# A hybrid encoder layer on one core: half of branch C's output gate is projected later, between the merges of two branches

## The chip, the cores and the metric

One core of one Trainium2 chip runs one launch of the kernel. The metric is the device time in microseconds (us), the median of several runs. TensorE is called PE, VectorE DVE, ScalarE ACT, GpSimd POOL and SyncE SP, as in the profile.

## The reference, cut to what matters

One encoder layer over 512 tokens of width 1024, in float32. A normed input n is projected once; three token mixers (A: sparse attention, B: stick-breaking attention, C: gated linear attention) work on the columns; their outputs are merged under sigmoid gates; a second block retrieves 16 experts for each of 8 heads and each token.

```python
# branch C: o is the output of the recurrence, r the columns cr of n @ w_in
o = rms_norm(o, out_gain) * jax.nn.silu(r)
...
merged = gates[:, :, 0] * (ya @ w_oa) + gates[:, :, 1] * (yb @ w_ob) + gates[:, :, 2] * (yc @ w_oc)
return merged @ w_out
...
# the expert block, for each block of 128 tokens
u = u_tab[expert]
vv = v_tab[expert]
act = gelu(einsum('nd,nhkd->nhk', xb, u))
out = einsum('nhk,nhkd->nd', g * act, vv)
```

The change concerns r, the output gate of branch C: 512 columns, 1024 inputs, 512 tokens. It is needed only as silu(r), multiplied into the normed output of branch C.

## The kernel before, in words

The order of the work is written out by hand, engine by engine. There are two stages.

**The front** runs until the first expert rows are fetched. PE projects n through a list of jobs (`jobs_of_projection`, one job being eight matmuls of 128x512, line 662 for jobs with tokens in the columns, line 664 for jobs with tokens in the rows). The last jobs of the list are four for r (name "rc", one for each 128 tokens) and two for the forget gates ("cu", line 675). A job number J_A on is interleaved with the heads of branch A: `job_after(it)` puts one behind every second step `it`, and the last LATE = 4 jobs stand behind the first scores of branch B (line 805). Between the last heads of A stand also the column sums of the modulation (`column_sums`, line 598) at `it == NA + 1`, and the turn of A's output (line 748). ACT copies every job's result out of PSUM, then applies Silu to all of rc (line 1380); POOL multiplies it by the output gain (line 2200); DVE multiplies branch C's normed output by it (line 1867). After branch C, PE merges the three branches for tokens 0 to 255 (`gate_product` line 769, `out_product` line 783), projects the merged columns (`output`, line 941) and turns tokens.

**The gather stage** works through NL = 512 expert rows for 128 tokens each. POOL fetches row n (1 MB) by an indirect DMA (line 2227) into a ring of 8 places, later 10 and more; DVE takes the dot product (line 2060), ACT the Gelu and a diagonal matrix (lines 1492 and 1503), PE adds the weighted row to an accumulator (`weigh`, line 1111), except for the rows that DVE adds itself (line 2084). A place is free again when its row has been added. Four rows make a slot; there are 128 slots, and PE, ACT, DVE and SP hang the rest of the layer on them by tables of slot numbers:

- `MERGE_SLOT`: 24 merges for tokens 256 to 511 in slots 3 to 35. Merge n is `merge_products(n)` on PE (line 1013, eight matmuls of 128x256 for the gate; line 1018, four for the branch's output), `half_gate(n)` on ACT (a tanh), `half_merge(n)` on DVE (lines 1903 and 1907). Its weights (768 KB) come from SP (`merge_weights`, line 537) into one of three places.
- `PIECE_SLOT`: the output projection of these tokens (line 1037), slots 37 to 40, then the residual sum, the norm and its shift (ADD_AT 42 to SHIFT_AT 49; the shift is line 1576 on ACT).
- `LATE_QUERY_AT` (line 1047), `late_at` (attention of branch A for tokens 256 to 511, lines 1125, 1136, 1148) and `QUERY_SLOT` (expert queries, line 974, scores line 999, with 1152 KB of weights from SP, line 531).
- `KEPT_UNTIL`: the row from which two more ring places are used.

## Time and profile before

| what | value |
|---|---|
| median of 3 runs | 2058.62 us (2057.96 to 2058.76) |
| the profiled execution's own time | 2061.57 us |
| its span, first to last instruction | 2059.8 us |
| PE busy | 1671.6 us (81%) |
| DVE busy | 1457.2 us (71%) |
| ACT busy | 580.0 us (28%) |
| POOL busy | 616.0 us (30%) |
| bytes moved by DMA | 659.79 MB |
| mean granted PE clock | 0.913 of full |

The profiled execution is 1.8 us longer than its span and 3.0 us longer than the median. Shares of busy time are averages over two stages that have different limits, so the stage has to be read before the share is used. fp32 matmuls leave two records each: a job of eight matmuls has 16 records.

### The profile page before, as it was taken

The page shows a single profiled execution, that of the slowest core. Times are in us where ns is not written, and L with a number is a line of the kernel's source. Part 1 is how long each engine was busy: PE and PEld are TensorE (multiplying, and loading weights), DVE is VectorE, ACT ScalarE, POOL GpSimd, SP SyncE. Part 2 cuts the span into 40 slices and gives each one's busy share as a digit, 9 for nine tenths or more (in the row PEclk, how much of TensorE's full clock was granted, in tenths as well). Part 3 has the DMA queues.
Part 4 walks back from the last instruction along what each step waited for, and adds up shares of the span by engine and source line. Part 5 has one row for each costly group of instructions (what it writes and reads, how often), then busy time and mean ns, then how long its engine had stood idle before and what let it go on. Part 6 is the DMA issues. An engine that isn't in the chain of part 4 may idle for free.

```text
span 2059.8 us, 17894 instructions
## 1 busy us (share of the span) xinstructions
PE 1671.6 (81%) x5626; PEld 945.6 (46%) x5626; DVE 1457.2 (71%) x3371; ACT 580.0 (28%) x1272; POOL 616.0 (30%) x542
## 2 busy tenths in 40 slices
PE   4999999999898998998898667777887676666665
PEld 3533455667786665565555323333443222222222
DVE  5454642668328688877787998887777878887876
ACT  2121114664224443542222223222222222212221
POOL 0000000110003333333444445444443544344441
PEclk8999899999999999999999978888888888888988
DMA  9632120021448899999999999999999999999995
GB/s 371 247 125 89 70 102 9 31 92 62 169 163 353 336 401 417 397 403 401 412 401 419 420 419 383 420 419 420 420 419 421 420 420 419 420 419 420 420 420 243
DMA packets 89184, 659.79 MB, mean 320 GB/s; under 512 B 9968, under 2 KB 10240, under 8 KB 15488
## 3 DMA queue, kind: packets, MB, share of 16 engines
q0 software_dynamic: 73728, 536.90, 63.5%
q1 hardware_dynamic: 14768, 120.75, 14.7%
q8 instruction: 45, 0.74, 0.1%
q10 hardware_dynamic: 592, 0.98, 0.1%
q14 instruction: 51, 0.42, 0.1%
HBM read 655.52 MB, written 2.82 MB: 320 GB/s over the span
## 4 chain that ended last, share of the span: by engine, by line
DMA 39%; PE 34%; DVE 14%; issue 7%; ACT 4%; POOL 2%; SPq 0%; DVEq 0%; POOLq 0%; ACTq 0%
DMA sb<-uv_table,sb 36%; PE ps L1111 9%; PE ps L662 4%; PE ps L664 4%; DMA sb<-w_mod 3%; DVE sb L2060 3%; PE ps L769 3%; PE ps L974 2%; DVE sb L2084 2%; POOL sb L2227 2%; PE ps L1013 1%; PE ps L1018 1%; PE ps L941 1%; PE ps L783 1%; PE ps L634 1%
## 5 line engine op out<-in xcount | busy, mean ns | idle before, releaser
L1111 PE MATMUL ps<-sb 128*128 128x512 f32 x1424 | 767.7, 683 | 291.7 <-ACT sb L1503 286.9
L2227 POOL DMA_INDIRECT sb<-uv_table,sb x512 | 589.0, 1150 | 910.5 <-PE ps L1111 700.6
L2060 DVE CUSTOM_DVE_ANT_0 sb<-sb 128x1024 f32<-128x1024 f32 x512 | 625.2, 1221 | 250.3 <-DMA sb<-uv_table,sb 240.6
L1111 PEld LDWEIGHTS ps<-sb 128*128 128x128 f32 x1424 | 289.7, 216 | 717.4 <-ACT sb L1503 415.9
L1503 ACT ACTIVATE sb<-sb 128x128 f32<-128x128 f32 x356 | 132.0, 397 | 614.0 <-DVE sb L2069 607.1
L2084 DVE SCALAR_TENSOR_TENSOR sb<-sb 128x512 f32<-128x512 f32 x304 | 214.8, 748 | 2.2
L1492 ACT ACTIVATE sb<-sb 128x2 f32<-128x2 f32 x256 | 51.7, 202 | 400.1 <-DVE sb L2060 400.0
L2189 POOL TENSOR_TENSOR sb<-sb 128x128 f32<-128x128 f32 x8 | 13.1, 1636 | 427.3 <-DVE sb L1766 427.3
L662 PE MATMUL ps<-sb 128*128 128x512 f32 (+1 forms) x304 | 128.6, 576 | 0.1
L974 PE MATMUL ps<-sb 128*128 128x256 f32 (+1 forms) x576 | 123.6, 371 | 0.0
L974 PEld LDWEIGHTS ps<-sb 128*128 128x128 f32 x576 | 104.2, 204 | 29.6 <-issue 17.4
L769 PE MATMUL ps<-sb 128*128 128x256 f32 x384 | 89.9, 387 | 8.5 <-DVEq L1742 3.6
L664 PE MATMUL ps<-sb 128*128 128x512 f32 x192 | 90.3, 626 | 0.0
L662 PEld LDWEIGHTS ps<-sb 128*128 128x128 f32 x304 | 58.3, 198 | 64.2 <-issue 57.7
L1013 PE MATMUL ps<-sb 128*128 128x256 f32 x384 | 87.3, 379 | 0.0
L769 PEld LDWEIGHTS ps<-sb 128*128 128x128 f32 x384 | 71.9, 192 | 22.4 <-issue 7.4
L1013 PEld LDWEIGHTS ps<-sb 128*128 128x128 f32 x384 | 71.2, 189 | 15.1 <-issue 6.0
L1018 PE MATMUL ps<-sb 128*128 128x256 f32 x192 | 49.9, 405 | 13.7 <-DVE sb L1907 13.7
L664 PEld LDWEIGHTS ps<-sb 128*128 128x128 f32 x192 | 37.7, 201 | 47.5 <-issue 46.6
L1554 ACT ACT_TABLE_LOAD x43 | 55.2, 1283 | 0.8
L2069 DVE TENSOR_TENSOR sb<-sb 128x2 f32<-128x2 f32 x256 | 39.9, 156 | 16.8 <-ACT sb L1492 15.1
L1018 PEld LDWEIGHTS ps<-sb 128*128 128x128 f32 x192 | 37.7, 200 | 22.6 <-DVE sb L1907 16.9
(283 smaller groups left out, 1784.9 us busy)
## 6 DMA issues: line engine op xcount, KB each, us to landing
sb<-w_mod SPq DMA_DIRECT2D x11, 2048.0 KB, 9.2
sb<-w_pq SPq DMA_DIRECT2D x18, 1152.0 KB
sb<-w_merge SPq DMA_DIRECT2D x24, 768.0 KB
sb<-w_proj SPq DMA_DIRECT2D x8, 2048.0 KB, 8.8
sb<-w_merge SPq DMA_DIRECT2D x6, 2304.0 KB, 9.0
sb<-w_out SPq DMA_DIRECT2D x8, 1024.0 KB, 11.7
sb<-uv_table,sb POOLq DMA_INDIRECT x512, 27.8
sb<-w_merge SPq DMA_DIRECT2D x3, 1536.0 KB, 6.7
```

The costliest lines, as they stand in the source:

```text
L662: mm = pe.matmul(bank(b, n), w[:, i, k, :], n_t[:, k, 0:n], start=(k == 0), stop=(k == KT - 1))
L664: mm = pe.matmul(bank(b), n_t[:, k, P * i:P * (i + 1)], tiles(views[slot], KT)[:, k, :], start=(k == 0), stop=(k == KT - 1))
L769: mm = pe.matmul(gate_at(n), w[:, P * k:P * (k + 1)], n_t[:, k, 0:H], start=(k == 0), stop=(k == KT - 1))
L974: mm = pe.matmul(bank(6 if q < EARLY_Q else 4, n, H * c), w[:, c, k, :], n_t[:, k, lo:lo + n], start=(k == 0), stop=(k == KT - 1))
L1013: mm = pe.matmul(bank(6, H), w[:, P * k:P * (k + 1)], n_t[:, k, H:T], start=(k == 0), stop=(k == KT - 1))
L1018: mm = pe.matmul(bank(7, H), w[:, P * (KT + k):P * (KT + k + 1)], y_of(br, 1)[:, k, :], start=(k == 0), stop=(k == 3))
L1111: mm = pe.matmul(bank(2 * (t % 2) + f), dgw[m % NDG], row_v(n)[:, T * f:T * (f + 1)], start=(i == 0), stop=(i == PH * PK - 2))
L1503: act.activation(dgw[m % NDG], ident, ACT.Copy, scale=wgt[n // PK % 2][:, n % PK:n % PK + 1])\
L1554: act.activation(warm, cact[:, 0:1], ACT.Gelu)
L2060: dve.tensor_tensor_reduce(out=row_u(n), in0=row_u(n), in1=n2_tm(u // PH), scale=1.0, scalar=0.0, op0=ALU.mult, op1=ALU.add, accum_out=dot ...
L2084: ins = dve.scalar_tensor_tensor(acc_v[f], v, wgt[u % 2][:, i:i + 1], acc_v[f], ALU.mult, ALU.add)
L2227: pool.indirect_dma_start(out=ring[PLACE[n]], out_offset=None, in_=uv_table, in_offset=bass.IndirectOffsetOnAxis(ap=experts[u % 4][:, i:i ...
```

## The change

- Jobs of rc: two instead of four (tokens 0 to 255). The list is two shorter, so no job stands behind steps 17 and 19 of branch A any more, and the four late jobs are rc 0, rc 1 and the two cu jobs. Silu, the gain and DVE's product cover half the columns.
- For tokens 256 to 511 r is computed transposed in the gather stage: `ITEMS` is eight merges of branch B, four items "gate", eight merges of C, eight of A. A gate item is eight matmuls of 128x256 on PE, a tanh on ACT, and two operations on DVE, which multiply branch C's output in place. Its weights are 512 KB from a new input w_rc; the 2 MB of the front's load are as before.
- The 28 items stand in slots 4 to 37, and what follows them moves by two or three slots. The late queries and branch A's late attention move by two slots. Expert query 10 moves from slot 29 to 44, query 11 from 51 to 53.

```diff
-    jobs += [("t", 7, t, "rc", None) for t in range(TT)]
+    jobs += [("t", 7, t, "rc", None) for t in range(TT // 2)]
...
-        KEPT_UNTIL = 116
+        KEPT_UNTIL = 120
...
-        QUERY_SLOT = {4 * (q - 3) + 1: q for q in range(3, 11)}
-        QUERY_SLOT.update({(51 if q == 11 else 4 * q + 9): q for q in range(11, NQ)})
+        QUERY_SLOT = {(44 if q == 10 else 4 * (q - 3) + 1): q for q in range(3, 11)}
+        QUERY_SLOT.update({(53 if q == 11 else 4 * q + 9): q for q in range(11, NQ)})
...
-        def half_unit(n):
-            return (n // KT + 1) % 3, n % KT
+        ITEMS = [(1, c) for c in range(KT)] + [("gate", c) for c in range(4)] + [(2, c) for c in range(KT)] + [(0, c) for c in range(KT)]
+        NM = len(ITEMS)
...
         def late_at(j):
-            return 1 + j + (3 if j >= HA else 0)
+            return 3 + j + (3 if j >= HA else 0)
...
-            [3, 4, 7, 8, 11, 12, 15, 16, 19, 20, 21, 22, 23, 24, 26, 27, 28, 29, 30, 31, 32, 33, 34, 35])}
-        PIECE_SLOT = {37 + p: p for p in range(4)}
-        TURN_SLOT = {25: (6, 7), 46: (8, 9), 48: (10, 11), 53: (12, 13), 54: (14, 15)}
-        G2_SLOT = 28
-        LATE_QUERY_AT = {0: 2, 2: 3}
-        LATE_SQ_AT, LATE_VAR_AT, LATE_ROOT_AT, LATE_R_AT = 3, 4, 5, 6
-        ADD_AT, SQUARE_AT, SUM_AT, NVAR_AT, ROOT_AT, NORM_AT, SHIFT_AT = 42, 42, 44, 47, 47, 49, 49
-        ONES_AT = 45
+            [4, 6, 7, 8, 11, 12, 14, 15, 16, 18, 19, 20, 22, 23, 24, 25, 26, 27, 28, 29, 30, 31, 32, 33, 34, 35, 36, 37])}
+        PIECE_SLOT = {39 + p: p for p in range(4)}
+        TURN_SLOT = {27: (6, 7), 48: (8, 9), 50: (10, 11), 55: (12, 13), 56: (14, 15)}
+        G2_SLOT = 29
+        LATE_QUERY_AT = {2: 2, 4: 3}
+        LATE_SQ_AT, LATE_VAR_AT, LATE_ROOT_AT, LATE_R_AT = 5, 6, 7, 8
+        ADD_AT, SQUARE_AT, SUM_AT, NVAR_AT, ROOT_AT, NORM_AT, SHIFT_AT = 44, 44, 46, 49, 50, 52, 52
+        ONES_AT = 47
...
+                if br == "gate":
+                    sp.dma_start(mh_slot[n % 3][:, 0:KT * P], w_rc[:, KT * P * c:KT * P * (c + 1)]).then_inc(mh_in[n % 3], 16)
...
                 pe.wait_ge(s["gate_ready"], NG + n)
+                if n >= 1 and ITEMS[n - 1][0] == "gate":
+                    pe.wait_ge(s["gate_used"], NG + n)
...
+                if br == "gate":
+                    pe.wait_ge(s["gl_done"], NG + n + 1)
+                    pe.sem_inc(s["ob_done"], 1)
+                    pe.sem_inc(s["mh_used"], 1)
+                    return
...
-            act.activation(area("rc", 0, TT * T), area("rc", 0, TT * T), ACT.Silu).then_inc(s["rsil"], 1)
+            act.activation(area("rc", 0, 2 * T), area("rc", 0, 2 * T), ACT.Silu).then_inc(s["rsil"], 1)
...
+                if br == "gate":
+                    y = y_of(2, 1)[:, c, :]
+                    done(dve.scalar_tensor_tensor(gates_h[n % 2], gates_h[n % 2], 1.0, bank(6, H), ALU.add, ALU.mult))
+                    dve.scalar_tensor_tensor(y, y, vcol(V_OGC + c), gates_h[n % 2], ALU.mult, ALU.mult).then_inc(s["gate_used"], 1)
```

PE at the end of branch A and the start of branch B, before the change (line 664 is a job of rc, 598 the column sums, 748 the turn of A's output, 805 the first scores of B, 675 the jobs of cu):

```order
L739 MATMUL ps<-sb 128x64 x4
L664 MATMUL ps<-sb 128x512 x8
L598 MATMUL ps<-sb 128x1 x32
L748 MATMUL ps<-sb 128x128 x4
L664 MATMUL ps<-sb 128x512 x8
L805 MATMUL ps<-sb 128x512
L805 MATMUL ps<-sb 128x384
L805 MATMUL ps<-sb 128x256
L805 MATMUL ps<-sb 128x128
L664 MATMUL ps<-sb 128x512 x16
L675 MATMUL ps<-sb 128x512 x2
```

The same place in the changed kernel, whose lines are two to four numbers further on:

```order
L742 MATMUL ps<-sb 128x64 x4
L601 MATMUL ps<-sb 128x1 x32
L751 MATMUL ps<-sb 128x128 x4
L808 MATMUL ps<-sb 128x512
L808 MATMUL ps<-sb 128x384
L808 MATMUL ps<-sb 128x256
L808 MATMUL ps<-sb 128x128
L667 MATMUL ps<-sb 128x512 x16
L678 MATMUL ps<-sb 128x512 x2
```

One job ahead of the column sums and one ahead of B's first scores are gone; behind the scores stand 16 matmuls as before.

PE in slots 0 to 3 of the gather stage, before the change (1111 weighs rows, 1047 is a late query of A, 974 half an expert query, 999 its scores, 1013 and 1018 a merge, 1125 late scores of A):

```order
L1111 MATMUL ps<-sb 128x512 x12
L1047 MATMUL ps<-sb 128x256 x8
L974 MATMUL ps<-sb 128x256 x8
L1111 MATMUL ps<-sb 128x512 x2
L1125 MATMUL ps<-sb 128x384
L974 MATMUL ps<-sb 128x256 x8
L1047 MATMUL ps<-sb 128x256 x8
L1111 MATMUL ps<-sb 128x512 x6
L1125 MATMUL ps<-sb 128x384
L999 MATMUL ps<-sb 128x128 x4
L1056 MATMUL ps<-sb 128x2 x4
L1013 MATMUL ps<-sb 128x256 x8
```

And changed (1123 weighs, 1059 is a late query, 979 half an expert query, 1004 its scores, 1020 and 1030 a merge, 1137 late scores):

```order
L1123 MATMUL ps<-sb 128x512 x12
L979 MATMUL ps<-sb 128x256 x8
L1123 MATMUL ps<-sb 128x512 x2
L979 MATMUL ps<-sb 128x256 x8
L1059 MATMUL ps<-sb 128x256 x8
L1123 MATMUL ps<-sb 128x512 x6
L1004 MATMUL ps<-sb 128x128 x4
L1123 MATMUL ps<-sb 128x512 x4
L1137 MATMUL ps<-sb 128x384
L1059 MATMUL ps<-sb 128x256 x8
L1020 MATMUL ps<-sb 128x256 x8
L1030 MATMUL ps<-sb 128x256 x4
```

One late query, the first merge and three late scores no longer stand ahead of the weighing of slot 3 (the x4 in the middle of the second piece).

## Rows read from the trace of the kernel before

**Rows 1.** The page, the span in 40 slices: DMA share in tenths, GB/s
```profile
DMA  9632120021448899999999999999999999999995
GB/s 371 247 125 89 70 102 9 31 92 62 169 163 353 336 401 417 397 403 401 412 401 419 420 419 383 420 419 420 420 419 421 420 420 419 420 419 420 420 420 243
```

**Rows 2.** Busy by stretch: span, PE, PEld, DVE, ACT, POOL, clock, DMA share, GB/s
```profile
300.00:400.00 100.00, 94.28 (x362) 61.53 (x361) 39.15 (x60) 48.47 (x47) 10.25 (x12) 0.95 0.09 34
...
700.00:1100.00 400.00, 364.57 (x1376) 235.62 (x1375) 316.26 (x799) 134.42 (x313) 147.73 (x132) 0.97 1.00 405
```

**Rows 3.** The chain that ended last, end of A and start of B: start, us, what
```profile
297.58 6.94 PE ps L664 x16
304.51 9.84 PE ps L598 x64
314.35 0.95 PE ps L748 x4
315.31 8.59 PE ps L664 x16
...
323.92 0.61 ACT sb L1249
...
324.66 2.39 PE ps L805 x8
327.05 13.97 PE ps L664 x32
```

**Rows 4.** Busy by stretch, around the column sums, columns as in rows 2
```profile
304.00:314.00 10.00, 10.00 (x65) 9.76 (x64) 0.00 (x0) 0.60 (x1) 0.00 (x0) 0.72 0.01 2
...
315.00:320.00 5.00, 5.00 (x10) 2.21 (x9) 0.07 (x1) 0.60 (x1) 0.00 (x0) 0.64 0.00 0
```

**Rows 5.** Busy by stretch, slots 0 to 3, columns as in rows 2
```profile
650.00:660.00 10.00, 6.14 (x8) 2.52 (x8) 9.62 (x36) 3.98 (x11) 2.61 (x2) 0.66 0.90 359
660.00:670.00 10.00, 10.00 (x40) 7.09 (x38) 9.93 (x30) 4.69 (x11) 3.19 (x3) 1.00 0.92 343
670.00:680.00 10.00, 10.00 (x40) 7.46 (x40) 5.30 (x17) 2.59 (x7) 0.77 (x2) 1.00 0.37 129
680.00:690.00 10.00, 10.00 (x48) 7.29 (x46) 6.02 (x12) 2.87 (x6) 4.92 (x5) 1.00 0.81 315
```

**Rows 6.** Timelines of PE and POOL there: start, us, instruction, idle before
```profile
660.45 3.62 PE L1047 MATMUL ps<-sb 128*128 128x256 f32 x16
...
677.02 5.32 PE L1111 MATMUL ps<-sb 128*128 128x512 f32 x12
...
679.68 1.41 POOL L2227 DMA_INDIRECT sb<-uv_table,sb  x1 [9.23 <-PE ps L1111]
```

**Rows 7.** The page, groups: a merge's gate and output products
```profile
L1013 PE MATMUL ps<-sb 128*128 128x256 f32 x384 | 87.3, 379 | 0.0
L1018 PE MATMUL ps<-sb 128*128 128x256 f32 x192 | 49.9, 405 | 13.7 <-DVE sb L1907 13.7
```

**Rows 8.** Busy by stretch, behind the norm of tokens 256 to 511
```profile
1250.00:1260.00 10.00, 8.98 (x18) 3.95 (x17) 9.83 (x27) 1.30 (x4) 4.75 (x4) 0.64 0.73 257
```

**Rows 9.** The page, DMA queues: packets, MB, share of 16 engines
```profile
q1 hardware_dynamic: 14768, 120.75, 14.7%
```

**Rows 10.** Busy by stretch, one with weights from SP, columns as in rows 2
```profile
860.00:870.00 10.00, 10.00 (x39) 5.97 (x38) 8.97 (x27) 5.49 (x12) 3.93 (x4) 1.00 0.99 373
```

**Rows 11.** DMA issues: KB each, median us to landing
```profile
kept<-sb ACTq DMA_DIRECT2D x2, 256.0 KB, 4.7
```

**Rows 12.** Waits of PE from 690 to 1130 us: us in total, times, longest
```profile
PE ps L1018 <- DVE sb L1907: 13.7, 8, 2.9
```

**Rows 13.** Timeline of POOL, the first fetch of an expert row
```profile
619.58 1.11 POOL L2227 DMA_INDIRECT sb<-uv_table,sb  x1 [95.91 <-DVEq L2054]
```

More of the change, by code:

```diff
@@ L41 @@
 C_END = C_FUTURE + 128
-V_C, V_BMOD, V_G1, V_G2, V_BG, V_BA, V_GAIN, V_ONG = 0, 8, 56, 64, 72, 96, 98, 102
+V_C, V_BMOD, V_G1, V_G2, V_BG, V_BA, V_GAIN, V_OGC, V_ONG = 0, 8, 56, 64, 72, 96, 98, 102, 106
 V_END = V_ONG + HC * CV
@@ L533, in merge_weights @@
             def merge_weights(n):
-                br, c = half_unit(n)
+                br, c = ITEMS[n]
                 if n >= 3:
                     sp.wait_ge(s["mh_used"], n - 2)
-                sp.dma_start(mh_slot[n % 3], w_merge[3 * br + c // 3][:, UNIT_W * (c % 3):UNIT_W * (c % 3 + 1)])\
-                  .then_inc(mh_in[n % 3], 16)
+                if br == "gate":
+                    sp.dma_start(mh_slot[n % 3][:, 0:KT * P], w_rc[:, KT * P * c:KT * P * (c + 1)]).then_inc(mh_in[n % 3], 16)
+                else:
+                    sp.dma_start(mh_slot[n % 3], w_merge[3 * br + c // 3][:, UNIT_W * (c % 3):UNIT_W * (c % 3 + 1)])\
+                      .then_inc(mh_in[n % 3], 16)
             def out_weights(p):
@@ L561, in _ @@
             for slot in range(NL // GROUP):
-                if slot in MERGE_SLOT and MERGE_SLOT[slot] + 3 < NG:
+                if slot in MERGE_SLOT and MERGE_SLOT[slot] + 3 < NM:
                     merge_weights(MERGE_SLOT[slot] + 3)
@@ L568, in _ @@
                     sp.dma_start(area("x", KT * H, KT * H), x_turned[:, KT * H:2 * KT * H]).then_inc(s["ld_x2"], 16)
-                if slot == 36:
-                    sp.wait_ge(s["mh_used"], NG)
+                if slot == 38:
+                    sp.wait_ge(s["mh_used"], NM)
                     out_weights(0)
@@ L971, in query @@
                         pe.wait_ge(s["sc_out"], q)
+                    if q == 10:
+                        pe.wait_ge(s["yg_ready"], 8)
                 w = pq_slot[:, 0:2 * D].rearrange("p (i k n) -> p i k n", i=2, k=KT)
@@ L1003, in merge_products @@
             def merge_products(n):
-                br, c = half_unit(n)
+                br, c = ITEMS[n]
                 w = mh_slot[n % 3]
@@ L1027, in output_piece @@
                 if p == 0:
-                    pe.wait_ge(s["gate_used"], 2 * NG)
+                    pe.wait_ge(s["gate_used"], NG + NM)
                     pe.wait_ge(s["ot_out"], TT)
-                    pe.wait_ge(s["q_out"], 11)
-                    pe.wait_ge(s["sc_out"], 11)
+                    pe.wait_ge(s["q_out"], 10)
+                    pe.wait_ge(s["sc_out"], 10)
                 if p >= 2:
@@ L1444, in half_gate @@
                     act.wait_ge(s["gate_used"], NG + n - 1)
-                br, c = half_unit(n)
-                act.activation(gates_h[n % 2], bank(6, H), ACT.Tanh, scale=0.5, bias=half_bias[:, KT * br + c:KT * br + c + 1])\
-                   .then_inc(s["gate_ready"], 1)
+                br, c = ITEMS[n]
+                bias = 0.0 if br == "gate" else half_bias[:, KT * br + c:KT * br + c + 1]
+                act.activation(gates_h[n % 2], bank(6, H), ACT.Tanh, scale=0.5, bias=bias).then_inc(s["gate_ready"], 1)
             def gated_piece(p):
@@ L1732, in _ @@
             dve.tensor_scalar(half_bias, vcol(V_BG, NG), 0.5, None, ALU.mult)
+            done(dve.tensor_scalar(vcol(V_OGC, 4), vcol(V_OGC, 4), 0.5, None, ALU.mult))
             dve.tensor_scalar(half_gt1, mcol(GT1, KT), 0.5, None, ALU.mult).then_inc(s["halved"], 1)
@@ L1864, in _ @@
             for b in range(2):
-                e = c_e[:, 2 * T * b:2 * T * (b + 1)].rearrange("p (t a v) -> p t a v", t=TT, v=CV)
-                g = area("rc", 0, TT * T).rearrange("p (t a b v) -> p t a b v", t=TT, b=2, v=CV)[:, :, :, b, :]
+                e = c_e[:, 2 * T * b:2 * T * (b + 1)].rearrange("p (t a v) -> p t a v", t=TT, v=CV)[:, 0:2]
+                g = area("rc", 0, 2 * T).rearrange("p (t a b v) -> p t a b v", t=2, b=2, v=CV)[:, :, :, b, :]
                 ins = dve.tensor_tensor(e, e, g, ALU.mult)
@@ L1896, in half_merge @@
             def half_merge(n):
-                c = n % KT
+                br, c = ITEMS[n]
                 dve.wait_ge(s["gate_ready"], NG + n + 1)
@@ L2260, in laid_out @@
          col(d["c_b_alpha"][0])] + [np.tile(d[k][0], 2)[:, None] for k in ("a_qn_g", "a_kn_g", "b_qn_g", "b_kn_g")]
-        + [np.tile(d["c_on_g"][0], (P, 1))], 1)
+        + [col(np.ravel(d["c_on_g"][0])), np.tile(d["c_on_g"][0], (P, 1))], 1)
     small = np.concatenate([av, iw, ca], 1)
@@ L2267, in laid_out @@
         "w_small": by_row(small), "w_alpha": d["c_w_alpha"][0], "w_merge": np.stack(merge),
-        "w_out": by_tile(d["w_out"][0]), "w_pq": pq,
+        "w_out": by_tile(d["w_out"][0]), "w_rc": by_tile(cr), "w_pq": pq,
         "uv_table": np.concatenate([d["peer_u"][0], d["peer_v"][0]], 1),
```

6 lines of the change are left out of this document (3 added, 3 removed).

## The prediction

> **What bounds the kernel now.** I read the page's slices first, because the shares of the whole span mix two stages. The reader should see a break in the DMA line: almost idle in the middle of the front, then 9 from about slice 14 to the end, at 400 to 421 GB/s [rows 1]. So the kernel is two stages in series. In the gather stage the 16 DMA engines are the bound: from 700 to 1100 us their share is 1.00 although PE is busy 364.57 us of the 400 [rows 2], and the later slices hold 419 or 420 GB/s. There an engine's work costs nothing as long as DMA does not run dry; bytes cost, and so does every stretch in which DMA idles. In the front it is the reverse: from 300 to 400 us DMA has a share of 0.09 and PE is busy 94.28 of 100 us [rows 2]. The chain of waits confirms it: around 300 us it is made of PE pieces that follow each other with gaps under a microsecond [rows 3].
>
> **The change, part by part.**
>
> *The front loses two projection jobs.* Before, from the end of branch A's last product to the first scores of B, the chain reads: a job of rc 6.94 us, the column sums 9.84, the turn 0.95, a second job of rc 8.59, a short wait on ACT, then the scores at 324.66 [rows 3]. That is 324.66 - 297.58 = 27.1 us. Of the two jobs nothing is left there. Behind the scores the two other jobs (13.97 us) are replaced by rc 0 and rc 1, which are of the same size, so the cover that they give to ACT and DVE in B's first head stays. What comes to light is the copy of A's turned output on ACT, which the second job hid and for which the scores wait: the copy beside it is 0.61 us [rows 3], with signals about 0.8. The new stretch is 9.84 + 0.95 + 0.8 = 11.6 us, so 15.5 us go.
>
> Not all of that is kept. The granted clock is 0.72 on average during the column sums and still 0.64 in the five microseconds behind them [rows 4], between the two levels of 1.2 and 2.4 GHz. The job behind them took 8.59 us in the chain and the job ahead of them 6.94 [rows 3]: 1.65 us were lost to the low clock, and that loss moves to the scores and to rc 0. The net gain is 15.5 - 1.65 = 13.9 us. If the low level lasts longer because the short scores and a wait now stand there, another 1.4 may go, and if the copy is fully covered 0.8 come back: 12.5 to 14.7.
>
> *Silu, gain and product on half the columns* are costed at nothing: the product of DVE ends while PE works on gate products that do not need it, and ACT and POOL finish before. Behind rc the front is a chain of PE, ACT and DVE that moves as a whole; its loads from SP are not late, DMA having a share of 0.09.
>
> *Slots 0 to 3 become lighter.* Between 650 and 690 us DMA idles 1.0 + 0.8 + 6.3 + 1.9 = 10 us [rows 5]. The cause is PE: POOL waited 9.23 us for a weighing before it could issue the next fetch at 679.68, while PE did late queries and expert queries; the six matmuls of slot 2 began only at 677.02 [rows 6]. In the changed order one late query (3.62 us [rows 6]) and one late score no longer stand ahead of them, and slot 3 is weighed without a merge (3.6 + 2.1 us, 87.3/24 and 49.9/24 [rows 7]) ahead of it. Fetches are released 3 to 10 us earlier, but DVE is busy 9.62 and 9.93 of 10 us from 650 to 670 [rows 5] and holds part of it back. Bounds: nothing, or all of the 10 us. I take 4, which is the late query that leaves the place where POOL waited.
>
> *The 28 items in slots 4 to 37.* The four gate items add 4 x 3.64 = 14.6 us of PE, and query 10 (two halves like those of 3.6 us) leaves for slots 44 to 46, where PE has time. PE's idle time from 700 to 1100 us is 400 - 364.57 = 35.4 us [rows 2]. That is more than twice the additional work, so I cost it at nothing; with the cover gone each gate item would cost its 3.64 us and its wait. The last merge moves from slot 35 to 37, and one slot is four fetches; pieces, norm and shift follow at the same distances, and their deadline (the queries of tokens 256 to 511) moves with them.
>
> *The dip behind the norm.* In one stretch DMA has a share of 0.73, with DVE at 9.83 of 10 us [rows 8]: the norm of tokens 256 to 511 and picks of experts stand in the same slot. In the new table norm and shift fall in slot 52, whose first rows carry no picks, but query 11 follows one slot behind instead of two. Bounds: the 2.7 us gone, or doubled. I take a gain of 1.
>
> *Bytes.* The front's load is unchanged, so 4 x 512 KB = 2.10 MB are added, all in the stage where DMA is the bound. SP's queue moved 120.75 MB in 14.7% of 2059.8 us [rows 9], which is 2.51 us for each MB: 5.3 us. Not less than 2.10 MB at 420 GB/s, 5.0 us. For the upper end: in a stretch with weights from SP the rate is 373 at a share of 0.99, against 419 in the later slices [rows 1, 10]; 10 us at 46 GB/s less are 0.46 MB or 1.1 us for a load, and four of them with their bytes make 9.7 us. I take 5.3, since the queue's own row includes all sizes.
>
> **Sum**, against the profiled execution's 2061.57: -13.9 - 4 - 1 + 5.3 = -13.6, so 2048.0. It lies 2.95 us over the median of the runs; the median forecast is **2045 us**. About 0.2% (4.1 us) is what a measurement of this kernel can tell from no change.
>
> **The rivals.**
>
> *The early idle time vanishes whole.* With slots 0 to 3 light, DMA might never run dry: -13.9 - 10 - 2.7 + 5.3 = -21.3, a median of 2037. For it: PE was the engine waited for at every late fetch there. Against it: DVE is full until 670 us. Chance 0.15.
>
> *The loads cost more than their bytes.* Each of the four small loads holds the engines back as in [rows 10]: 9.7 instead of 5.3, and 2049. The Trainium skill ("DMA: Bandwidth & Descriptors", "Anatomy of one DMA") gives 2.0 us fixed for a DMA beside its bytes at 436 GB/s. By that rule, an estimate from this page, four loads would be 12.8 us and the median 2052; the trace speaks against it as a sum, as fetches overlap and DMA stays at 1.00 with over a hundred of them in a row. Chance 0.13.
>
> *The front's gain is swallowed.* DVE may start B only when penalties of A have been written to DRAM by ACT, after the turn; this write is issued 15 us earlier now, but if it or a load arrives late, B's first head waits and the front gives nothing: 0 - 4 - 1 + 5.3 = 0.3, 2059, no change. Against it: the transfers land in 4.7 us at the median [rows 11], about as long as ACT's first three operations of B need. Chance 0.08.
>
> *Slower: PE becomes the bound of slots 4 to 37.* A gate item keeps its PSUM bank until ACT's tanh and two DVE operations are through, and the next item waits for that at its start, no longer between its halves. The like wait is now 13.7 us in all, up to 2.9 once [rows 12]. If PE is the bound, each gate item costs 3.64 + 2.9 us, four 26 us, and +26 - 13.9 + 5.3 = +17.6 gives 2076. It decides from the point at which the 35.4 us of PE idle time are used up and DMA's share falls below 0.95 between 750 and 1100 us. Chance 0.04.
>
> **How the numbers follow.** The forecast has 0.60. Its own range is 2041 to 2050, from the bounds 12.5 to 14.7, 2 to 7 and 5.0 to 9.7. Faster than by 0.2%: 0.60 + 0.15 + 0.13 = 0.88; within it 0.08; slower 0.04. The range that leaves out no more than 2 in 10 reaches from the first rival's 2037 to 2054, where the low ends of the gains meet the high price of the bytes (-12.5 - 2 + 9.7 = -4.8, so 2054).
>
> **What the changed profile would show.** The gap between A's last product and B's first scores at 12 us instead of 27; the first fetch at about 605 to 606 us instead of 619.58 [rows 13]; the job behind the scores slower than 7 us by 1 to 2; DMA idle between there and steady state down from 10 to about 6 us; SP's queue at 122.8 MB; a share of 0.99 to 1.00 and no less than 400 GB/s until the last merge. A first fetch later than 609 refutes the front's term; a DMA share under 0.95 between 750 and 1100 us makes the slower rival true; a rate well below 400 GB/s around slots 13 to 20 the dearer loads.

## The result: 0.3% slower, and the profile after

| what | value |
|---|---|
| changed kernel, median of 22 runs | 2060.97 us (2054.73 to 2068.86) |
| kernel before, on the same chip, median of 22 runs | 2055.64 us (2048.52 to 2059.51) |
| ratio, with its 95% interval | 1.0031 (1.0021 to 1.0042) |
| forecast | 2045.0, range 2037 to 2054, faster 0.88 |
| profiled execution after: own time, span | 2060.94, 2059.1 us |
| profiled execution before: own time, span | 2061.57, 2059.8 us |

The forecast was wrong: 14 us faster was expected, and the kernel became 5 to 6 us slower. The two profiled executions have the same length, which is itself misleading: the end of one and the same front turned out to differ by 6 to 10 us between profiled executions (below), and the one shown of before was a slow draw, with the latest first fetch of ten.

**The front.** The chain that ended last, end of A and start of B, after (start, us, what), beside [rows 3]:

```profile
283.42 6.95 PE ps L665 x16
...
292.20 10.31 PE ps L601 x64
302.51 0.97 PE ps L751 x4
...
303.50 0.61 ACT sb L1313
...
304.15 4.63 PE ps L808 x8
308.78 15.94 PE ps L667 x32
```

From the end of A's last product (292.20) to the scores of B (304.15) it is 11.95 us, where before it was 27.1; 11.6 were forecast. But the scores and the two jobs behind them now take 4.63 + 15.94 = 20.6 us, against 2.39 + 13.97 = 16.4 [rows 3]: 4.2 us are given back, not 1.65. The granted clock over the scores is 0.50, where before it was 1.00. It stands at 0.50 from 296 to 311 us, that is through most of the column sums, the turn, the scores and the start of the first job; before, it stood there from 310 to 318 us and was back at 1.00 before the scores. The timeline of POOL has the first fetch 15.9 us earlier than [rows 13]:

```profile
603.72 1.11 POOL L2244 DMA_INDIRECT sb<-uv_table,sb  x1 [99.27 <-DVEq L2071]
```

**The gather stage.** The page, the span in 40 slices after, beside [rows 1]:

```profile
DMA  9632210112649999999999999999999999999995
GB/s 371 247 125 105 98 67 0 60 63 78 238 165 353 393 402 395 377 358 399 417 418 416 416 409 387 415 419 419 419 419 420 419 419 419 419 419 419 419 418 239
```

Slices 16 and 17, counted from 0 (823 to 926 us), moved 377 and 358 GB/s, where before they moved 397 and 403. Busy by stretch there, columns as in [rows 2]; first the kernel before:

```profile
800.00:900.00 100.00, 92.50 (x340) 57.77 (x339) 80.79 (x207) 46.10 (x95) 33.67 (x33) 0.97 1.00 405
```

and the changed kernel:

```profile
700.00:1100.00 400.00, 363.71 (x1361) 237.06 (x1360) 310.12 (x787) 133.79 (x308) 145.79 (x125) 0.96 0.98 394
800.00:900.00 100.00, 86.75 (x306) 54.05 (x305) 73.25 (x190) 35.04 (x77) 30.25 (x28) 0.91 0.92 360
...
870.00:880.00 10.00, 9.55 (x32) 7.06 (x33) 3.69 (x7) 5.01 (x9) 0.79 (x1) 0.70 0.80 315
...
890.00:900.00 10.00, 9.70 (x47) 6.02 (x46) 5.32 (x19) 3.21 (x8) 4.36 (x4) 1.00 0.78 270
```

From 800 to 900 us DMA idles 8% of the time and *every* engine is less busy than before, PE too (86.75 for 92.50). That is no overloaded engine; it is engines that wait for each other. (A second profile of the kernel before, x1 below, has a share of 0.96 there, so a few hundredths of it say nothing by themselves.) The timeline of PE shows where (start, us, instruction, idle before and who ended it):

```profile
865.73 1.16 PE L1004 MATMUL ps<-sb 128*128 128x128 f32 x8
870.14 6.53 PE L1020 MATMUL ps<-sb 128*128 128x256 f32 x16 [3.25 <-DVE sb L1918]
876.98 1.96 PE L1123 MATMUL ps<-sb 128*128 128x512 f32 x4 [0.30 <-PE ps L1020]
...
886.00 5.38 PE L1020 MATMUL ps<-sb 128*128 128x256 f32 x16 [3.00 <-DVE sb L1918]
891.68 1.96 PE L1123 MATMUL ps<-sb 128*128 128x512 f32 x4 [0.30 <-PE ps L1020]
```

The gate products of two items (L1020, x16 each) wait 3.25 and 3.00 us at their head for DVE's second operation on the gate item before (L1918), which gives the PSUM bank back, and then run at a lowered clock (0.70 from 870 to 880 us, 0.72 from 886 to 892): 6.53 and 5.38 us instead of 3.64. Behind them stand the weighings (L1123), and the ring's places come free with these. POOL's timeline shows the next fetches held up:

```profile
879.22 0.94 POOL L2244 DMA_INDIRECT sb<-uv_table,sb  x1 [11.67 <-PE ps L1123]
...
893.91 0.94 POOL L2244 DMA_INDIRECT sb<-uv_table,sb  x1 [9.41 <-PE ps L1123]
```

And DVE's timeline shows why it came late: it had itself waited for PE, and then had the late attention's sums (L1932), two dot products (L2077), a row of its own to add (L2101) and the picks of experts (L2032 to L2041) ahead of the half merge. The first and the last of these operations are:

```profile
861.46 0.69 DVE L1932 CUSTOM_DVE_ANT_0 sb<-ps,sb 128x512 f32<-128x512 f32 x1 [4.43 <-PE ps L1148]
...
868.60 0.23 DVE L2041 TENSOR_SCALAR sb<-sb 128x16 f32<-128x16 f32 x1
869.05 0.42 DVE L1917 SCALAR_TENSOR_TENSOR sb<-sb,ps 128x256 f32<-128x256 f32 x1 [0.22 <-DVE sb L2041]
869.51 0.49 DVE L1918 SCALAR_TENSOR_TENSOR sb<-sb 128x256 f32<-128x256 f32 x1
```

The page's groups, gate and output products after, beside [rows 7]; L1013, which is L1020 in the old kernel, had no idle time before it:

```profile
L1020 PE MATMUL ps<-sb 128*128 128x256 f32 x448 | 106.2, 392 | 6.8 <-DVE sb L1918 6.3
...
L1030 PE MATMUL ps<-sb 128*128 128x256 f32 x192 | 51.5, 415 | 16.5 <-DVE sb L1924 14.5
```

A tally of the fetches shows the course: fetch 16 (slot 4) is issued 20.6 us earlier than in the profile of before, so the light slots 0 to 3 give another 4.7 to the front's 15.9; fetch 72 (slot 18) 19.1 us earlier, fetch 88 (slot 22) only 4.6, fetch 152 (slot 38, behind the last merge) 5.9, the last fetch 1.4. The slots 18 to 38 lost 13 us.

That the light slots gain 4 us holds in all 20 profiles of this document: from fetch 0 to fetch 16 it is 57.3 to 60.3 us, mean 59.3, in the six with the late work in its old slots, and 52.8 to 56.2, mean 55.3, in the fourteen that have it two slots later.

### The profile page after: what moved, and what is told of

Same layout as the page of the kernel before. It is cut to its first block, busy times and chain, and to the rows that moved or that the text cites. A ratio compares the mean times of both kernels' runs of the same rounds, so it can differ in the third digit from the quotient of the medians.

```text
span 2059.1 us, 17992 instructions
## 1 busy us (share of the span) xinstructions
PE 1681.4 (82%) x5658; PEld 961.8 (47%) x5658; DVE 1460.3 (71%) x3380; ACT 578.9 (28%) x1274; POOL 625.2 (30%) x542
## 3 DMA queue, kind: packets, MB, share of 16 engines
q1 hardware_dynamic: 15344, 122.85, 15.2%
## 4 chain that ended last, share of the span: by engine, by line
DMA 36%; PE 36%; DVE 15%; issue 7%; ACT 4%; POOL 2%; SPq 0%; DVEq 0%; POOLq 0%; ACTq 0%
DMA sb<-uv_table,sb 33%; PE ps L1123 10%; PE ps L665 4%; DMA sb<-w_mod 3%; PE ps L667 3%; PE ps L979 3%; PE ps L772 3%; DVE sb L2077 3%; DVE sb L2101 2%; PE ps L1020 2%; POOL sb L2244 2%; PE ps L1030 1%; PE ps L944 1%; PE ps L786 1%; PE ps L1049 1%
## 5 line engine op out<-in xcount | busy, mean ns | idle before, releaser
L1123 PE MATMUL ps<-sb 128*128 128x512 f32 x1424 | 769.5, 686 | 276.1 <-ACT sb L1515 271.3
L2244 POOL DMA_INDIRECT sb<-uv_table,sb x512 | 600.4, 1173 | 916.6 <-PE ps L1123 700.6
L2077 DVE CUSTOM_DVE_ANT_0 sb<-sb 128x1024 f32<-128x1024 f32 x512 | 625.6, 1222 | 253.8 <-DMA sb<-uv_table,sb 246.8
L1123 PEld LDWEIGHTS ps<-sb 128*128 128x128 f32 x1424 | 290.4, 216 | 696.3 <-ACT sb L1515 395.2
L2101 DVE SCALAR_TENSOR_TENSOR sb<-sb 128x512 f32<-128x512 f32 x304 | 214.9, 749 | 2.2
L979 PEld LDWEIGHTS ps<-sb 128*128 128x128 f32 x576 | 103.7, 204 | 31.4 <-issue 20.3
L1020 PE MATMUL ps<-sb 128*128 128x256 f32 x448 | 106.2, 392 | 6.8 <-DVE sb L1918 6.3
L1020 PEld LDWEIGHTS ps<-sb 128*128 128x128 f32 x448 | 86.9, 196 | 27.3 <-issue 15.2
L772 PE MATMUL ps<-sb 128*128 128x256 f32 x384 | 90.0, 388 | 8.5 <-DVEq L1755 3.7
L665 PEld LDWEIGHTS ps<-sb 128*128 128x128 f32 x304 | 58.7, 199 | 62.9 <-issue 56.8
L772 PEld LDWEIGHTS ps<-sb 128*128 128x128 f32 x384 | 72.1, 192 | 22.4 <-issue 7.5
L667 PE MATMUL ps<-sb 128*128 128x512 f32 x160 | 74.2, 620 | 0.0
L1030 PE MATMUL ps<-sb 128*128 128x256 f32 x192 | 51.5, 415 | 16.5 <-DVE sb L1924 14.5
L1030 PEld LDWEIGHTS ps<-sb 128*128 128x128 f32 x192 | 38.2, 204 | 26.8 <-DVE sb L1924 18.3
L667 PEld LDWEIGHTS ps<-sb 128*128 128x128 f32 x160 | 31.2, 199 | 39.4 <-issue 38.6
L1649 DVE SCALAR_TENSOR_TENSOR sb<-sb 128x4096 f32<-128x4096 f32 x7 | 31.4, 4483 | 22.0 <-DMA sb<-w_mod 21.9
```

The costliest lines, as they stand in the source:

```text
L665: mm = pe.matmul(bank(b, n), w[:, i, k, :], n_t[:, k, 0:n], start=(k == 0), stop=(k == KT - 1))
L667: mm = pe.matmul(bank(b), n_t[:, k, P * i:P * (i + 1)], tiles(views[slot], KT)[:, k, :], start=(k == 0), stop=(k == KT - 1))
L772: mm = pe.matmul(gate_at(n), w[:, P * k:P * (k + 1)], n_t[:, k, 0:H], start=(k == 0), stop=(k == KT - 1))
L979: mm = pe.matmul(bank(6 if q < EARLY_Q else 4, n, H * c), w[:, c, k, :], n_t[:, k, lo:lo + n], start=(k == 0), stop=(k == KT - 1))
L1020: mm = pe.matmul(bank(6, H), w[:, P * k:P * (k + 1)], n_t[:, k, H:T], start=(k == 0), stop=(k == KT - 1))
L1030: mm = pe.matmul(bank(7, H), w[:, P * (KT + k):P * (KT + k + 1)], y_of(br, 1)[:, k, :], start=(k == 0), stop=(k == 3))
```

## The experiments

Two theories stood against each other at the start. **The gate items**: the forecast's front and table are right in kind, and the four gate items with their loads cost what they gained. The expectations call it W where the wait at the start of the next item is the cost, and L where PE's work is. **The table** (T): the new slot numbers lose by themselves. Later a third was added, **the place** (P): the 4 new columns of constants move every tile behind them.

**The kernel before once more (x1), as a measure of the front.**

> The kernel before once more, with a second profile: is its profiled execution (2061.57 us, above the 2055.64 median of 22 runs) an ordinary one? If so the second profile's DMA share is again 0.99 to 1.00 from 700 to 1100 us, with idle DMA time of 10 to 12 us before 700 us, and the ratio is 1.000. If single executions differ by up to 10 us, the place where they differ should show in the fetch times of the rows.

Measured: 2052.98 us, 0.9994 (0.9977 to 1.0011). Its chain at the same place:

```profile
283.64 6.95 PE ps L662 x16
...
292.43 6.94 PE ps L664 x16
299.36 10.48 PE ps L598 x64
309.85 0.95 PE ps L748 x4
310.80 7.92 PE ps L664 x16
...
319.49 2.39 PE ps L805 x8
321.88 13.97 PE ps L664 x32
```

The same program is here at 299.36 at the column sums, and was at 304.51 in [rows 3]. Single jobs of the projection account for it. The one below took 1.7 us longer in the first execution, at a granted clock of 0.81 where x1 had 1.00; another 3.3 us were lost between 203 and 226 us, where the clock was 0.73 on average (200 to 225 us) and 0.86 in x1. The job at the same place of the program in the two timelines of PE, first the execution shown above, then x1:

```profile
194.59 8.84 PE L664 MATMUL ps<-sb 128*128 128x512 f32 x16
```

```profile
194.44 7.15 PE L664 MATMUL ps<-sb 128*128 128x512 f32 x16
```

So the first fetch of one profiled execution can't give the front's gain. All 20 profiles can: with the old front it is issued at 613.6 to 619.6 us, mean 616.5 (10 profiles); with the new one at 600.4 to 610.4, mean 605.5 (10 profiles). The front gained **11 us**, an estimate with some 3 us of uncertainty from this spread.

The changed stretch by itself varies far less. From the end of A's last product to the end of the two jobs behind the scores, the ten profiles with the new front have 32.5 us each (to within 0.1), and eight of the ten with the old front 43.4 (x5 and x6 have 45.1). That is a gain of 10.9 us, and the scores take 4.63 us in all ten of the new and 2.39 in all ten of the old.

**Gate items in alternating banks (x2).**

```
+        def gbank(n):
+            return 7 if ITEMS[n][0] == "gate" and ITEMS[n][1] % 2 else 6
-                if n >= 1 and ITEMS[n - 1][0] == "gate":
-                    pe.wait_ge(s["gate_used"], NG + n)
+                if n >= 1 and "gate" in (ITEMS[n - 1][0], br):
+                    pe.wait_ge(s["gate_used"], NG + n - 1)
```

> The changed kernel, but the gate items alternate between PSUM banks 6 and 7, so that the item behind one no longer waits at its start for DVE to read the bank. Theory W (the wait at the head of the item, 3.25 and 3.0 us in the changed profile, and the low clock behind it cost what was lost between slots 16 and 24): 6 to 9 us faster than the changed kernel, about 2053 or a ratio of 0.998 to 0.999 to the kernel before. Theory L (the load of PE in slots 14 to 25 costs, whoever waits for whom): within 2 us of the changed kernel, 2060, ratio 1.002. Theory T (the new table of slots costs by itself): as L.

Measured: 0.9997 (0.9985 to 1.0008), 0.0034 or 7 us (4 to 10) below the changed kernel: the gain that W expected. No wait for DVE at the head of an item is left, and from 800 to 900 us DMA is back at 0.99 (in x8 below, the same kernel at another offset, it is 0.97):

```profile
L1023 PE MATMUL ps<-sb 128*128 128x256 f32 x448 | 101.6, 379 | 0.9 <-ACT sb L1462 0.9
```

```profile
800.00:900.00 100.00, 90.41 (x334) 56.24 (x333) 79.93 (x206) 38.87 (x86) 36.78 (x32) 0.95 0.99 393
```

**The changed kernel without its gate items and their loads (x3).**

```
-        ITEMS = [(1, c) for c in range(KT)] + [("gate", c) for c in range(4)] + [(2, c) for c in range(KT)] + ...
+        ITEMS = [(1, c) for c in range(KT)] + [(2, c) for c in range(KT)] + ...
-            [4, 6, 7, 8, 11, 12, 14, 15, 16, 18, 19, 20, 22, ...
+            [4, 6, 7, 8, 11, 12, 14, 15, 22, ...
```

> The changed kernel without its four gate items and their loads (branch C of tokens 256 to 511 is left without its output gate); slots 16, 18, 19, 20 are empty, all else stays. My prediction had the gate items at 5.3 us, for their bytes alone: then this is 2055 or 0.999. Theories W and L, in which the items cost their bytes and 11 to 14 us more: 2042 to 2045, ratio 0.994 to 0.995. Theory T: 2055 or more, since the table stays.

This kernel leaves out branch C's output gate for tokens 256 to 511. Measured: 0.9955 (0.9940 to 0.9970). The four items with their loads cost 1.0031 - 0.9955 = 0.0076, or **15.6 us** (12 to 19). The forecast had 5.3.

**The changed kernel without their loads alone (x9).**

```
-                if br == "gate":
-                    sp.dma_start(mh_slot[n % 3][:, 0:KT * P], w_rc[:, KT * P * c:KT * P * (c + 1)]).then_inc(mh_in[n % 3], 16)
-                else:
+                if br != "gate":
```

> The changed kernel without the four transfers of w_rc: its gate items multiply with whatever weights lie in their places, all their work and waits stay. This prices the bytes. The prediction had 5.3 us: 2055.5 to 2056, ratio 1.0005 (the changed kernel: 1.0031). If each load costs more than its bytes (9.7 us): 1.000 or below, 0.9985. If DMA was not the bound where the gate items stand, because the wait on DVE let it idle: less than 3 us, 1.002 to 1.003.

Measured: 1.0010 (0.9994 to 1.0026), 0.0021 or **4.3 us** below the changed kernel; the interval reaches from 0 to 8. With the 7 us of the bank, 15.6 - 7.0 - 4.3 = 4.3 us remain for PE's, ACT's and DVE's work on the items; this last part is what is left over, it was not measured by itself, and bank and bytes were each taken out alone and not together.

The profiles give the same picture at the place itself. The gate items stand in slots 16 to 20, and what they delay shows in the fetches of slots 16 to 25. From fetch 64 to fetch 100, by POOL's timelines:

| kernel | us |
|---|---|
| changed kernel | 115.8 |
| without the loads (x9) | 112.6 |
| alternating banks (x2, x8) | 108.4, 109.9 |
| without gate items and loads (x3) | 101.1 |

That is 14.7 us for the items, of which 6 to 7 go with the bank's wait and 3 with the loads. Single profiles of this stretch differ by some us: the three kernels without gate items and with the old front (x4, x7, x15, next) have 102.2 to 106.5.

**The old front with the new table (x4), and the same at the old place of the constants (x7, x15).** x4 keeps all of rc in the front and places 24 merges in slots 4, 6, 7, 8, 11, 12, 14, 15 and 22 to 37. It has the 4 columns of the changed kernel; x7 and x15, one kernel, do not.

> The kernel before with the changed kernel's table of slots alone: r is computed whole in the front, no gate items, 24 merges in slots 4 to 15 and 22 to 37. Prediction's terms for the table: 4 us from slots 0 to 3 and 1 us from the dip, so 2050 to 2051, ratio 0.9975. Theory T (the table costs: late attention, queries and sixteen items in a row from slot 22): 2058 to 2062, ratio above 1.001. Theories W and L: as the prediction.

> x4 (the new table of slots, r whole in the front, no gate items) without the four columns: the table alone. Theory T: still 1.002 to 1.003, as x4's 1.0027. Theory P: 1.000 or, with the 4 to 5 us that the prediction gives the table, 0.998.

> The kernel of x7 once more (new slot table, 24 merges, old place of the constants; merges in 4 to 15 and 22 to 37), beside x13 and x14 on one chip: x7 gave 1.0007 with an interval too wide to tell from nothing. If the packed merges cost, 1.001 to 1.002; if the table is neutral, 0.999 to 1.000; the 0.998 that the forecast of 4 + 1 us asks for would say that x7 was a bad draw.

Measured: x4 1.0027 (1.0014 to 1.0040), x7 1.0007 (0.9991 to 1.0023), x15 1.0011 (0.9997 to 1.0025). The forecast of the table, 4 + 1 us, would be 0.9976, and is outside all three. The mean of x7 and x15 is 1.0009: **+2 us**. x4 lies 4 us above it. The place of its tiles does not explain that (x5 and x8 below), so it stays open, and with x4 counted in the table costs 3 us. x3, which differs from x4 by the new front alone, lies 0.0072 or 15 us below it, and 0.0054 or 11 us below the mean of x7 and x15. Of these two the trace supports the 11 (10.9 us in the changed stretch). Front -11, table +2 and gate items +15.6 make +6.6, where the ratio 1.0031 is 6.4 us. These three close by the way they are formed, x3 and the mean standing in two of them each; what is independent is that the front comes out at 11 in the profiles too.

**The second half of the table alone (x13), and a looser first half (x14).**

```
-            [3, 4, 7, 8, 11, 12, 15, 16, 19, 20, 21, 22, 23, 24, 26, 27, 28, 29, 30, 31, 32, 33, 34, 35])}
+            [4, 6, 7, 8, 11, 12, 15, 16, 19, 20, 21, 22, 23, 24, 26, 27, 30, 31, 32, 33, 34, 35, 36, 37])}
```

> The kernel before with the second half of its table alone in the new places: output pieces and everything behind them two slots later, query 10 behind the merges, query 11 in slot 53, the turns moved with them; the slots 0 to 36, with 24 merges, as in the kernel before but for query 10. If the table's cost sits in the later tail (pieces, norm and shift later, fewer slots of slack for the last queries), 1.001 to 1.002. If this half is neutral and the cost sits in the packing of the merges or in the light slots 0 to 3, 0.999 to 1.000.

> x13 with two things more: late queries and late attention two slots later, so that slots 0 to 2 are light as in the changed kernel, and the 24 merges in a looser row, with single free slots left in it (4, 6, 7, 8, 11, 12, 15, 16, 19 to 24, 26, 27, 30 to 37). If the light first slots gain what was forecast and the packing loses it, x14 is 0.002 (4 us) below x13 and x15 above both. If the gain of the light slots is given back whatever the packing, x14 is within 0.001 of x13 and of x15.

Measured: x13 0.9991 (0.9976 to 1.0006), x14 **0.9976** (0.9962 to 0.9991), on one chip with x15. So the later tail costs nothing that can be measured. Light first slots with merges that leave gaps give 5 us (2 to 8), the size of the forecast, though x14 is below x13 by only 0.0015, which the intervals don't separate. The same with branch C's and A's merges in sixteen consecutive slots, 22 to 37, is 0.0035 or 7 us (3 to 11) dearer than x14. Busy by stretch from 850 to 1020 us; first x14:

```profile
850.00:1020.00 170.00, 151.86 (x617) 98.92 (x616) 136.68 (x348) 61.80 (x140) 62.01 (x57) 0.99 1.00 405
```

and x15:

```profile
850.00:1020.00 170.00, 150.26 (x596) 98.07 (x595) 135.37 (x343) 61.92 (x140) 58.24 (x53) 0.94 0.98 394
```

x15 waits more for half merges and late attention there, less for ACT's diagonals, and has the lower clock (0.94 for 0.99). The table of waits of PE in this stretch (us in total, times, longest), x14:

```profile
PE ps L1113 <- ACT sb L1505: 12.5, 6, 4.5
PE ps L1020 <- DVE sb L1909: 4.0, 2, 2.6
```

and x15:

```profile
PE ps L1030 <- DVE sb L1919: 11.2, 5, 4.9
PE ps L1137 <- DVE sb L1927: 6.0, 3, 3.1
PE ps L1123 <- ACT sb L1515: 4.1, 2, 2.7
```

The loss sits in slots 25 to 30: from fetch 100 to fetch 120 it is 71.1 us in x15 and 61.4 in x14. What in those slots costs it was not separated. x14 does not only leave slots 25, 28 and 29 free of merges, it also starts C's merges three slots earlier, and slot 25 holds expert query 9 too. Packing alone is not enough for it: x11 and x12 below have the same sixteen merges in slots 22 to 37, x11 with 71.5 us in that stretch and x12, whose late attention stands two slots earlier, with 59.4.

**The place of the tiles (x5, x6, x8, x10).** The constants `vec` lie ahead of all other tiles; 4 more columns shift these by 16 bytes, from 24 to 40 bytes behind a multiple of 64, counted from the start of the kernel's one SBUF tensor. x5 is the kernel before with 4 unused columns, x6 with 10, which puts the tiles at multiples of 64 bytes; x8 is x2 moved to 24 bytes behind a multiple of 64, as before; x10 is the changed kernel at multiples of 64. The edit, in x6:

```
-V_C, V_BMOD, V_G1, V_G2, V_BG, V_BA, V_GAIN, V_ONG = 0, 8, 56, 64, 72, 96, 98, 102
+V_C, V_BMOD, V_G1, V_G2, V_BG, V_BA, V_GAIN, V_ONG = 0, 8, 56, 64, 72, 96, 98, 112
```

> The kernel before with four unused columns in its vector table, as the changed kernel's output gain adds them: every tile behind it lies 16 bytes further on in SBUF, and nothing else changes. Theory P (placement: the ring's places start at another offset, and the fetches run at 419 GB/s where the kernel before had 420, 0.2% of some 1400 us): 2 to 5 us slower than before, ratio 1.001 to 1.0025, and 419 in the late stretches. Theory T (the 5.6 us of x4 came from the slots): 1.000 and 420.

> The kernel before with ten unused columns: every tile behind the vector table starts at a multiple of 64 bytes. Theory P: a rate other than 420 GB/s in the late stretches and a ratio other than 1.000; faster if whole 64-byte lines are what counts. Theory T: 1.000.

> x2 (changed kernel with the gate items on alternating banks) with twelve more unused columns, so that all tiles behind the vector table have the offset within 64 bytes that they have in the kernel before. Theory P: 2 to 5 us faster than x2, ratio 0.9975 to 0.9985, and 420 GB/s. Theory T: as x2, 0.9997.

> The changed kernel with six unused columns, so that all tiles behind the vector table start at a multiple of 64 bytes. If x6's gain (1.15%, 427 instead of 420 GB/s) is one of the DMA rate and nothing else, it must come back here: 0.9885 x 1.0031, so 0.990 to 0.993. If it was a property of the kernel before alone, the ratio stays near 1.003.

Measured: x5 0.9998 (0.9987 to 1.0010) and x8 1.0002 (0.9985 to 1.0019): the 16 bytes are no part of the result that can be measured (by x5, no more than 2 or 3 us). x6 **0.9885** (0.9861 to 0.9908) and x10 0.9901 (0.9879 to 0.9924): at multiples of 64 bytes the whole kernel is 1.1 to 1.3% faster. The work is the same, the rate of the transfers is not. Busy by stretch in the steady part, before:

```profile
1310.00:1650.00 340.00, 255.11 (x644) 127.02 (x644) 269.71 (x680) 77.25 (x215) 155.89 (x130) 0.86 1.01 420
```

and x6:

```profile
1310.00:1650.00 340.00, 261.21 (x637) 126.67 (x635) 270.49 (x682) 78.83 (x222) 154.34 (x133) 0.85 1.01 427
```

The same busy share, 420 GB/s at the one place and 427 at the other. Over this stretch all seven profiled kernels at multiples of 64 have 427, and the other thirteen 419 or 420. Some 1400 us at 1.7% more are 24 us; 2057.1 (before, same chip) less 2033.35 are 23.8.

**Both mends together, and the light slots taken out of them (x11, x12).** x11 is x2 at multiples of 64 bytes. x12 puts its late queries and late attention back into the old slots, with the rows that belong to them:

```
-            return 3 + j + (3 if j >= HA else 0)
+            return 1 + j + (3 if j >= HA else 0)
-        LATE_QUERY_AT = {2: 2, 4: 3}
+        LATE_QUERY_AT = {0: 2, 2: 3}
```

> x2 (alternating banks) with the same six columns. Alignment and banks both: 0.9885 x 0.9997, so 0.987 to 0.990. With a faster DMA the stage can become more bound by PE, and then the gain of alignment is smaller than x6's: above 0.990.

> x11 with the late queries and branch A's late attention back in the slots of the kernel before (and KEPT_UNTIL 116); the 28 items stay in slots 4 to 37. Theory M (the 4 us gained in slots 0 to 3 were lost again in slots 4 to 14 because the late work was only moved there): no difference to x11, within 0.001. Theory T (late work of 512 columns and merges in the same slots 22 to 26 costs): 3 to 6 us faster than x11, 0.985 to 0.987. If the light slots 0 to 3 are worth their 4 us net: slower than x11 by 0.002.

Measured: x11 0.9878 (0.9859 to 0.9897), 0.0023 below the version with the wait (x10), in the direction of x2, though the intervals overlap. x12 0.9939 (0.9920 to 0.9957): with 28 items the two slots of delay are worth 0.0061 or 12.5 us (7 to 18), more than the 4 that the forecast gave them. In x12's profile fetch 16 comes 4.6 us later after fetch 0 than in x11's, and the fetches from 16 to 64 (slots 4 to 15) take another 7 us. The late work returns in the slots that the items need, and DMA from 800 to 900 us falls from 0.97 to 0.93:

```profile
800.00:900.00 100.00, 92.61 (x343) 58.75 (x342) 76.36 (x200) 44.34 (x91) 31.13 (x29) 0.93 0.93 372
```

**DVE's half of a merge two rows earlier (x16, x18).** What was left in x11 was PE's wait between the halves of an item, 16.2 us:

```profile
PE ps L1033 <- DVE sb L1927: 16.2, 6, 4.1
```

```
-                if i % 4 == 3 and n // GROUP - 1 in MERGE_SLOT:
+                if i % 4 == 1 and n // GROUP - 1 in MERGE_SLOT:
```

> x11 (changed kernel, gate items in alternating banks, tiles at multiples of 64 bytes) with DVE's half of a merge two rows earlier in the slot (row 1 of four instead of row 3). If what is left of the loss is PE waiting for DVE's product in bank 7, the waits of L1033 fall from 16 us to under 6 and the ratio from 0.988 to 0.985 or 0.986. If DVE, full itself, then waits for PE's products and tanh in its turn, 0.988 or above.

> The kernel of x16 once more, beside x17 on one chip; x16 had few runs and gave 0.9868 with an interval of 0.0020 to each side. 0.985 to 0.988 expected; in its profile the first fetch near 600 us, and no PE wait for DVE at the second half of a merge.

Measured: x16 0.9868 (0.9848 to 0.9888), x18 0.9855 (0.9834 to 0.9876). The wait is gone from both profiles, and the gain over x11 is 0.001 to 0.002, no more than the intervals: the wait did what the first expectation of x16 says, the time did not follow. In its place PE waits longer for ACT's diagonals, 7.3 us in x11 and 19.6 in x18 over the same stretch (620 to 1100 us):

```profile
PE ps L1126 <- ACT sb L1518: 19.6, 10, 4.1
```

**The mends with the old front (x17).** It has the tiles at multiples of 64 bytes, x14's table and the earlier half merge.

> The kernel before with three things that have gained alone: x14's loose table (0.9976), the tiles at multiples of 64 bytes (x6: 0.9885), and DVE's half of a merge two rows earlier (x16). The front is the old one and rc stays in it. If they add, 0.9976 x 0.9885 = 0.986, and 0.985 with the earlier merge: then moving half of rc out of the front buys nothing over what a looser table buys, since the 4 gate items and their bytes eat it. If moving rc still nets something, x18 is below x17 by 0.002 or more.

Measured: **0.9851** (0.9829 to 0.9872), 2029.1 us, beside 2029.47 of x18 on the same chip. So moving half of rc out of the front is worth nothing that can be measured between these two. They differ in more than the front and the four items, though: x18 still has its merges in consecutive slots, which cost 7 us in x15 against x14, and x17 has the looser table. Whether 28 items with gaps would let some of the front's 11 us through was not tried. The fastest version measured is the kernel before with tiles at multiples of 64 bytes, the looser table and the earlier half merge, 29 us (1.5%) faster than before.

## Why the prediction was wrong

**The front** (forecast -13.9, bounds 12.5 to 14.7; measured -11, by the first fetches of ten and ten profiles and by the changed stretch itself, 10.9). Right in mechanism and in the size of the gap: 11.95 for 11.6 us. The term that was mis-sized is the clock's, taken as the 1.65 us that one job lost before. The chain after has 4.2 us, 2.2 of them in the scores, which now run wholly at a granted clock of 0.50, and 2.0 in the two jobs. The text had weighed a longer low level at another 1.4, which is too little still. No run changed what stands there; that it is the wait on ACT and the short products that keep the clock low is argued, not shown.

**The 28 items at nothing** (measured 7 for the wait, some 4 for the rest; the step that failed). The argument was "PE's idle time from 700 to 1100 us is 35.4 us, more than twice the additional work". As cover for PE's own work it held for the larger part: of 14.6 us of additional matmuls some 4 reached the end, by the remainder above, which is uncertain by several us. What it left out is that an item also brings a wait, and that idle time consists of waits. The table of PE's waits from 620 to 1100 us in the changed kernel (us in total, times, longest):

```profile
PE ps L1030 <- DVE sb L1924: 14.5, 9, 3.4
PE ps L1123 <- ACT sb L1515: 8.0, 5, 3.9
PE ps L1137 <- DVE sb L1932: 6.5, 3, 4.7
PE ps L1020 <- DVE sb L1918: 6.3, 2, 3.3
```

The last line is new with the gate items. PE's work is written out in one order, and while it stands in this wait at the head of an item, the weighings behind it stand too, whatever idle time there is elsewhere. So the idle time was not used up, it is 400 - 363.71 = 36.3 us after, as large as before, and DMA's share still fell to 0.92 from 800 to 900. The mechanism was in the text, as the fourth rival: the bank that stays taken until DVE's second operation, waited for at the head of the item. It was given 0.04 because its price was tied to PE becoming the bound. Its mark came true from 800 to 900 us (0.92, though 0.98 over the whole of 700 to 1100), and its price was 15.6 us with bytes for all four items, not 26 + 5.3. The items behind two of the four gate items had to wait, 6.3 us in all, and the two products behind these waits ran 2.9 and 1.7 us longer at the lowered clock; 7 us reached the end (x2).

**Slots 0 to 3** (forecast -4; measured 4.7 at fetch 16, 4.0 over all profiles). Right, and right for the reason given. But slots 4 to 37 decide whether it stays: it does in the looser table (x14 0.9976) and does not with merges in consecutive slots (x15 1.0011). With 28 items the same delay is worth 12.5 us (x12 against x11). The forecast moved the items by count and did not ask what their spacing costs.

**The dip** (forecast -1). It moved from 1250 to the two windows from 1270 to 1290 us, with shares of 0.84 and 0.94: 2.2 us for 2.7. No term of any weight.

**Bytes** (forecast 5.3; measured 4.3 by x9, 0 to 8). Right as far as that goes: it can't tell 5.3 from less. The second rival, 9.7 for dearer loads, lies outside the interval. The Trainium skill ("DMA: Bandwidth & Descriptors", "Anatomy of one DMA — SWDGE (gpsimd) path") fits 2.0 us fixed beside the bytes for a single DMA issued by GpSimd, while these are issued by SyncE; four times that, an estimate from this page, was 12.8 us. x9 does not agree with such a sum: four loads amid the fetches of the ring cost 4.3 us together. SP's queue has the bytes forecast, and its share rose from 14.7% to 15.2%:

```profile
q1 hardware_dynamic: 15344, 122.85, 15.2%
```

**The third rival**, B's first head waiting for the write of the penalties, did not occur; the chain of the changed kernel shows no DMA in B's first head.

**The sum.** Forecast -13.9 - 4 - 1 + 5.3 + 0 = -13.6. Measured: -11 for the front, +2 for the table with packed merges in place of -5, 4.3 for bytes, 7 for the bank, 4.3 for the rest of the items, a remainder: +6.6. The three parts that failed are 2.9 (clock), 7 (table) and 11.3 (items at nothing); bytes gave 1.0 back. The range missed the time because these three had bounds of their own that left out what happened: 12.5 for the front, 2 for slots 0 to 3 (the text's own lower bound was nothing), and no price at all for the items. Two sums of the forecast don't follow from its terms: with 12.5, 2 and 9.7 and the dip's 1 its own range ends at 2053 and not at 2050, and the fourth rival's 2076 leaves out the gains of slots 0 to 3 and of the dip, with which it is 2071. Neither changes the outcome. Of the signs of being wrong, the DMA share under 0.95 pointed at the step that had failed. The one for dearer loads, a rate well below 400 GB/s, came true with it (360 from 800 to 900 us, the fetches of slots 16 to 22), though the loads were not the cause: x9, which has none, shows 358 there.

## What to carry to other kernels

Idle time of an engine is made of waits, so look up what it waits for before counting it as cover. Here it covered the larger part of 14.6 us of new matmuls, but not a new wait that came with them. When a step begins to need a buffer that the step before gives back last, price that wait and what is queued behind it in the same engine, down to the transfer that runs dry, whatever the engine's idle time. When work hung on a table of slots is moved, the gaps between its pieces can be part of its cost: sixteen merges in consecutive slots were 7 us dearer than the same merges with gaps and an earlier start. And take a front's gain from the changed stretch in several profiles, not from the time at which one profile ends it.
